# A product-key expert mixer: from gathered expert rows for all tokens to dense passes for three token tiles and gathered rows for two

## The chip, the cores and the metric

The kernel runs on one core of one Trainium2 chip. The metric is the device time of one execution in microseconds (us). Engines: PE (matrix multiply), DVE (VectorE), ACT (ScalarE), POOL (GpSimd), SP (issues DMAs).

## The reference, cut to what matters

The program is one step of a two-layer backbone over 640 tokens (128 context tokens, 512 latent tokens) of width 1024, all in float32. Each layer ends with an expert mixer over 16384 experts, each of which is one row of a table `u` and one row of a table `v`:

```
def peer(h, w_q, subkeys, u_tab, v_tab):
    q = (ht @ w_q).reshape(T, PEER_HEADS, 2, PEER_HALF)
    s = jnp.einsum('thpd,hpnd->thpn', q, subkeys)
    s1, i1 = lax.top_k(s[:, :, 0], PEER_TOPK)
    s2, i2 = lax.top_k(s[:, :, 1], PEER_TOPK)
    ...
    sc, pos = lax.top_k(cand, PEER_TOPK)
    eidx = jnp.take_along_axis(cidx, pos, axis=-1)
    gate = jax.nn.softmax(sc, axis=-1)
    def expert_block(args):
        xi, ei, gi = args
        a = jax.nn.gelu(jnp.einsum('td,tkd->tk', xi, u_tab[ei]), approximate=False)
        return jnp.einsum('tk,tkd->td', gi * a, v_tab[ei])
```

There are 8 heads, 128 keys per half (so expert = 128 i + j), and 16 experts per head: 128 picks per token, and 128 tokens per tile, 5 tiles. A row of either table is 4 KB, a whole table of one layer is 64 MiB (67.1 MB). The result is scaled by the layer's gate vector and added to the residual stream x.

## The kernel before, in words

The program is a row of stages (`build`), each closed by a barrier of all engines. In each layer the last two are `modulate` (normalises x into `h`, and PE turns `h` into `hT`) and `peer`. Everything outside `peer` is the same in both kernels but for one line of `modulate`.

`peer` of before works in 40 units, one for each tile and head. For one unit DVE chooses 16 experts per token: `select_subkeys` takes the best 16 of 128 scores for each half with `best16` (L1351 to L1355: MAX8, FIND_INDEX8, MATCH_REPLACE8, MAX8, FIND_INDEX8), and `select_experts` the best 16 of the 256 sums and their indices (L1363 to L1379). POOL then gathers rows (`gathers`, L1190 for u, L1194 for v): one indirect DMA fetches one row of 4 KB for each of the 128 tokens, 0.5 MB, into one of 8 slots for u and 8 for v. DVE multiplies each u row with the token's `h` and sums (`meet`, L1390), ACT applies the gelu, and DVE the gate (L1400). ACT makes a diagonal matrix of the 128 weights of each pick (L1240), and PE multiplies it with the gathered v rows and accumulates 16 picks in PSUM (`products`, L1303). DVE adds the sum to x (`add_y`, L1411 and L1414). The units are pipelined: the scores and the choice of unit n+1 lie in unit n. Most units are in hardware loops (`every`), in which each semaphore value is held in a register (`hold`).

Queries come first: PE turns the keys (L1330), and makes the queries of the context tile for all heads (L1338, weights loaded on SP in rows of 2 KB), and later the other 4 tiles' queries chunk by chunk between the products (L1313, weights `w_later` loaded on SP in rows of 512 bytes).

In all, each layer issues 640 gathers of u and 640 of v on POOL.

## Time and profile before

| | |
|---|---|
| median of 3 runs | 5233.46 us (5231.72 to 5237.55) |
| span of the profiled execution | 5232.4 us |
| its own time beside its span | shown nowhere but by the median: 1.1 us more |
| instructions | 51066 |
| busy PE, DVE, ACT, POOL | 3918.3, 3046.2, 1093.8, 3138.9 us |
| bytes read from HBM, written | 1476.98 MB, 3.48 MB |
| of these by POOL's gathers | 1342.42 MB, 2560 DMAs |

The trace is of one profiled execution. Busy time is the time in which an engine executes; a DMA's issue on POOL is counted as busy there. "PEclk" is the clock that PE was granted, 1.0 for 2.4 GHz and 0.5 for 1.2 GHz. "DMA share" is the mean busy share of the core's 16 DMA engines. "Releaser" is what ended an idle stretch of an engine; "issue" means that the profile shows nothing that it waited for.

### The profile page before, as it was taken

The numbers are of one execution on the slowest core, as the hardware profiler recorded it, in microseconds if no ns is written. First come the engines' busy times: TensorE is split into PE (matmuls) and PEld (weight loads), VectorE is DVE, ScalarE is ACT, GpSimd is POOL, SyncE is SP. The second block draws the span as 40 slices with busy tenths as digits, with TensorE's granted clock in tenths as the row PEclk, the third lists the DMA queues.
The fourth block names the chain that finished last, engine by engine and source line by source line (L and its number), as shares of the span: only waits on it lengthen the run. The fifth ranks groups of instructions, "written<-read, shape, count | busy, mean of one in ns | idle before, by whom it ended". The sixth has DMA issues, their size and how long they took to land. (4 is left out here: it accounts for less than half of the span.)

```text
span 5232.4 us, 51066 instructions
## 1 busy us (share of the span) xinstructions
PE 3918.3 (75%) x11340; PEld 1901.7 (36%) x11340; DVE 3046.2 (58%) x6901; ACT 1093.8 (21%) x2566; POOL 3138.9 (60%) x2832
## 2 busy tenths in 40 slices
PE   8986787787787666676678898877787666766675
PEld 3544754333333222232233443533333223322232
DVE  2014744766666666666651552666666666667665
ACT  1002212212221222122211242222222221222222
POOL 0003603777777777777760331477777777777775
PEclk9998888898898888888888799888889888888888
DMA  4126017999999999999992401899999999999997
GB/s 159 58 64 175 4 36 267 387 364 361 362 362 359 354 356 358 359 357 353 356 346 77 121 1 32 315 381 365 363 363 354 359 358 364 356 353 359 357 359 302
DMA packets 525836, 1482.66 MB, mean 283 GB/s; under 512 B 52901, under 2 KB 162597, under 8 KB 525513
## 3 DMA queue, kind: packets, MB, share of 16 engines
q0 software_dynamic: 369216, 1342.42, 68.7%
q1 hardware_dynamic: 154352, 138.22, 8.2%
q8 instruction: 58, 0.95, 0.1%
q14 instruction: 130, 1.06, 0.1%
q10 hardware_dynamic: 2080, 0.01, 0.0%
HBM read 1476.98 MB, written 3.48 MB: 283 GB/s over the span
## 5 line engine op out<-in xcount | busy, mean ns | idle before, releaser
L1303 PE MATMUL ps<-arena,mod_scale 128*128 128x512 f32 x5120 | 2472.0, 645 | 1030.4 <-ACT mod_scale L1240 1027.8
L1303 PEld LDWEIGHTS ps<-arena,mod_scale 128*128 128x128 f32 x5120 | 1051.5, 208 | 2414.9 <-issue 2324.7
L1190 POOL DMA_INDIRECT arena<-in_peer_u,small x1280 | 1381.3, 1079 | 726.3 <-issue 377.8
L1194 POOL DMA_INDIRECT arena<-in_peer_v,small x1280 | 1503.0, 1174 | 470.1 <-issue 317.8
L1390 DVE CUSTOM_DVE_ANT_0 arena<-arena 128x1024 f32<-128x1024 f32 x1280 | 1518.2, 1223 | 412.7 <-DMA arena<-in_peer_u,small 290.7
L1240 ACT ACTIVATE mod_scale<-ident,tail 128x128 f32<-128x128 f32 x1280 | 391.4, 388 | 82.3 <-DVE tail L1400 82.3
L1400 DVE TENSOR_TENSOR tail<-tail,small 128x8 f32<-128x8 f32 x160 | 27.0, 169 | 500.6 <-ACT tail L1236 499.9
L268 POOL TENSOR_TENSOR arena<-arena 2x512 f32<-2x512 f32 x12 | 15.5, 1294 | 464.4 <-ACT arena L260 464.4
L1236 ACT ACT_TABLE_LOAD x80 | 102.6, 1283 | 864.1 <-DVE tail L1390 863.9
L1228 ACT ACTIVATE arena<-ps 128x256 f32<-128x256 f32 x80 | 30.6, 382 | 1073.7 <-PE ps L1293 1073.7
L1313 PE MATMUL ps<-hT 128*128 128x512 f32 x512 | 231.6, 606 | 11.6 <-DMA hT<-in_peer_w_q 11.6
L1232 ACT ACT_TABLE_LOAD x80 | 102.6, 1283 | 560.3 <-DVE tail L1368 560.1
L527 PE MATMUL ps<-hT,arena 128*128 128x512 f32 x384 | 198.5, 599 | 2.1 <-PEq L70 2.1
L249 PE MATMUL ps<-hT,silu_c 128*2 128x128 f32 x1152 | 138.1, 280 | 43.9 <-DMA hT<-in_w_mod 43.0
L1785 POOL TENSOR_TENSOR arena<-arena,small 128x640 f32<-128x640 f32 (+3 forms) x80 | 76.2, 954 | 157.1 <-DVE small L1829 157.1
L1017 PE MATMUL ps<-arena,hT 128*128 128x512 f32 x320 | 141.8, 606 | 3.9 <-PEq L70 3.9
L1313 PEld LDWEIGHTS ps<-hT 128*128 128x128 f32 x512 | 97.1, 195 | 126.0 <-issue 110.8
L548 DVE COPY arena<-ps 128x640 f32<-128x640 f32 x12 | 9.9, 824 | 205.0 <-PE ps L528 205.0
L249 PEld LDWEIGHTS ps<-hT,silu_c 128*2 128x2 f32 x1152 | 95.8, 87 | 87.2 <-DMA hT<-in_w_mod 57.3
L1411 DVE TENSOR_TENSOR ps<-ps,mod_gate 128x1024 f32<-128x1024 f32 x80 | 98.5, 1231 | 41.8 <-PE ps L1303 32.7
L1351 DVE MAX8 small<-arena 128x8 f32<-128x128 f32 (+1 forms) x240 | 80.8, 337 | 65.3 <-ACT arena L1228 44.6
L1414 DVE TENSOR_TENSOR x<-x,ps 128x1024 f32 (+1 forms) x80 | 97.7, 1221 | 29.0 <-DVE ps L1411 28.6
(221 smaller groups left out, 3611.4 us busy)
## 6 DMA issues: line engine op xcount, KB each, us to landing
hT<-in_w_mod SPq DMA_DIRECT2D x144, 256.0 KB, 3.8
arena<-in_peer_u,small POOLq DMA_INDIRECT x1280, 6.3
arena<-in_peer_v,small POOLq DMA_INDIRECT x1280, 6.4
arena<-in_even_w_in SPq DMA_DIRECT2D x8, 2048.0 KB, 8.9
arena<-in_peer_w_q SPq DMA_DIRECT2D x8, 2048.0 KB, 11.6
hT<-in_peer_w_q SPq DMA_DIRECT2D x32, 512.0 KB, 15.0
arena<-in_w_mod SPq DMA_DIRECT2D x6, 2048.0 KB, 8.5
arena<-in_odd_w_in SPq DMA_DIRECT2D x3, 2048.0 KB, 14.1
```

The costliest lines, as they stand in the source:

```text
L249: mm = pe.matmul(self.m.ps[0:2, at % self.BANKS, c % 4 * P:(c % 4 + 1) * P], self.m.cT[:, k0 + k, :], self.ring[:, slot, k, :], start=(k0 ...
L527: pe.matmul(m.ps[:, b, :], lhsT, m.hT[:, k, 0:512], start=first, stop=end)
L1017: mm = pe.matmul(m.ps[:, i % 8, :], m.hT[:, k, t * P:(t + 1) * P], slots[n][:, k, :], start=(k == 0), stop=(k == KD - 1))
L1190: pool.indirect_dma_start(u_rows[:, j], None, u_table, at).then_inc(m.u_landed[j], 16)
L1194: pool.indirect_dma_start(v_rows[:, j], None, v_table, at).then_inc(m.v_landed[j], 16)
L1232: nc.scalar.activation(exps, sel, ACT.Exp, bias=neg_max, accum_out=exp_sum).then_inc(S.exp_ready, 1)
L1236: nc.scalar.activation(active[:, q], dots[:, q], ACT.Gelu).then_inc(S.gelu_ready, 1)
L1240: nc.scalar.activation(diag[:, q, j], m.ident[:], ACT.Copy, scale=weight[:, q, j:j + 1])\
L1303: mm = pe.matmul(y_banks[b][:, c], diag[:, q, j], v_rows[:, j, c * 512:(c + 1) * 512], start=(q == 0 and j == 0), stop=(q == 1 and j == HA ...
L1313: mm = pe.matmul(later_bank[i], w_later[:, k], m.hT[:, k, P:s.N], start=(k == 0), stop=(k == s.KD - 1))
L1390: dve.tensor_tensor_reduce(u_rows[:, j], u_rows[:, j], h_cur[:, b], 1.0, 0.0, ALU.mult, ALU.add, dots[:, q, j:j + 1]).then_inc(S.dotted, 1)
L1411: dve.tensor_tensor(share, share, mod, ALU.mult).then_inc(S.y_gated, 1)
```

## The change

`peer` is written anew. Tiles 0 and 1 (context and first latent tile) still go by gathered rows, 128 picks each, 256 picks per layer; tiles 2 to 4 (384 tokens) go dense over all 16384 experts, in 128 groups of 128 experts (group i holds experts 128 i + j). Both go on at once, interleaved in an order that is written out step by step (no loops are left, and all waits are on constants).

- **Prelude.** The queries of all five tiles are made 128 columns at a time by PE (`project`), followed by the scores (`score`) of all tiles; DVE chooses for tiles 0 and 1 (`choose`, `decode`). `decode` does for all 8 heads at once what was done per head.
- **First half, 128 steps in 4 stages of 32.** In step i SP loads 128 rows of u (4 DMAs of 32 partitions, rows of 1 KB), DVE transposes them in 32 x 32 blocks (`turn`), PE multiplies with `hT` of 384 tokens (`dots_of`), ACT applies the gelu and stores the 128 x 384 activations in DRAM (`act_rows`). In stages 0 to 2 DVE also makes one choice every 4 steps (tiles 2, 3, 4); at the start of stages 1 to 3 it decodes one tile; in stages 1 to 3 it makes, for 8 tokens at a time, one-hot matrices of i and j (`one_hot`, 128 x 1024 each, 48 groups), ACT multiplies one by the gate (`apply_gate`, 8 of 128 x 128), PE multiplies the two (`place_gates`), ACT copies the result out (`gates_out`), and stores it for two groups at a time, 1 MB, in DRAM (`gate_rows`).
- **Second half, 128 steps.** SP loads v (2 groups, 1 MB, rows of 4 KB), the activations (4 groups, rows of 1.5 KB) and the gates (8 groups, 1.6 MB, rows of 512 bytes); DVE multiplies activations by gates (`weigh`, 128 x 384), PE multiplies with v into 6 banks of PSUM (6 products of 128 x 512 a step).
- **Gathers beside both.** `pace` says how many picks are met by each step: 1.5 a step in stages 0 and 3, 0.25 in stages 1 and 2, 1.3 in the second half; the v rows follow 14 picks later. `meet` is as before. For tile 0 ACT scales each v row (`scale_row`) and POOL adds it; for tile 1 DVE does both in one (`add_row`). There are 8 slots for u and 4 for v. 512 gathers per layer.
- In `modulate` PE turns every eighth column of `h` instead of blocks of 128, and the query weights are loaded to match.

```diff
-                    mm = pe.transpose(m.ps[:, i % 8, j * P:(j + 1) * P], m.h[:, t, k * P:(k + 1) * P], m.ident[:])
+                    part = m.h[:, t, k * P:(k + 1) * P] if half == 0 else m.h[:, t, k::KD]
+                    mm = pe.transpose(m.ps[:, i % 8, j * P:(j + 1) * P], part, m.ident[:])
...
+LAG = 14
+def pace(i):
+    stage, r = divmod(i, STAGE)
+    if i < 0:
+        return 0
+    if stage == 0:
+        return max(0, 3 * (r - 1) // 2)
+    if stage in (1, 2):
+        return 45 + 8 * (stage - 1) + (r + 1) // 4
+    if stage == 3:
+        return 61 + 3 * (r + 1) // 2
+    return 109 + 13 * (i - STEPS + 1) // 10
...
+def rows_by(i):
+    return max(0, min(pace(i - 1) - LAG, P * GATHERED))
...
+            for k in range(PICKS + LAG):
+                if k + U_ROWS == P:
+                    pool.wait_ge(S.decoded, 2)
+                if k + U_ROWS < PICKS:
+                    pool.wait_ge(S.dotted, k + 1)
+                    u_gather(k + U_ROWS)
+                p = k - LAG
...
+                elif p < P:
+                    pool.wait_ge(S.scaled, p + 1)
+                    c(pool.tensor_tensor(y_sum[:, 0], y_sum[:, 0], v_rows[:, p % V_ROWS], ALU.add))
+                else:
+                    pool.wait_ge(S.dve_added, p - P + 1)
+                if p + V_ROWS < PICKS:
+                    v_gather(p + V_ROWS)
...
+                if n % 4 == 0:
...
+                    if g >= 2:
+                        sp.wait_ge(S.weighed, GBLOCK * (g - 1))
+                    sp.dma_start(g_in[:, g % 2].rearrange("p g i t -> p g (i t)"),
+                                 m.gate_rows[0:TG, :, g * GBLOCK:(g + 1) * GBLOCK, :].rearrange("g j i t -> j g (i t)"))\
+                        .then_inc(S.g_landed[g % 2], 16)
...
+                if n >= 2:
+                    sp.wait_ge(S.tile_done, VBLOCK * (n - 1))
+                sp.dma_start(v_in[:, n % 2], v_dense[n]).then_inc(S.v_landed[n % 2], 16)
...
+            for i in range(LAST):
+                if i + 2 < STEPS:
+                    turn(i + 2)
+                if i < STEPS:
+                    stage, r = divmod(i, STAGE)
+                    if stage >= 1 and r == 0:
+                        decode(GATHERED + stage - 1, best[0])
+                    for n in groups_at(i):
+                        one_hot(n)
+                    if head_at(i) is not None:
+                        t, h = head_at(i)
+                        choose(GATHERED + t, h, best[0])
+                if STEPS - 2 <= i < 2 * STEPS - 2:
+                    weigh(i - STEPS + 2)
+                for half in halves_by(i - 2):
+                    weights(half)
+                for p in range(picks_by(i - 1), picks_by(i)):
+                    meet(p)
+                for p in range(max(P, rows_by(i - 1)), max(P, rows_by(i))):
+                    add_row(p)
```

Three places of the order. First POOL in `peer` of the first layer. `L1190` and `L1194` are the gathers of u and v rows of before (`L1160` is the loop over units, `L1041` its register arithmetic):

```order
L1190 DMA arena<-in_peer_u,small 128x1024 x8
L1194 DMA arena<-in_peer_v,small 128x1024 x8
L1160 UNCONDITIONAL_BRANCH
L1160 ISA
L1041 ISA
L1190 DMA arena<-in_peer_u,small 128x1024
L1041 REGISTER_ALU
```

After the change, from the first gather on (`L1262` gathers u, `L1266` gathers v, `L1289` adds a scaled v row of tile 0 to the sum):

```order
L1262 DMA arena<-in_peer_u,small 128x1024 x8
L1266 DMA arena<-in_peer_v,small 128x1024 x4
L1262 DMA arena<-in_peer_u,small 128x1024 x15
L1266 DMA arena<-in_peer_v,small 128x1024
L1262 DMA arena<-in_peer_u,small 128x1024
L1289 TENSOR_TENSOR mod_shift<-mod_shift,arena 128x1024
L1266 DMA arena<-in_peer_v,small 128x1024
```

Runs of eight gathers have become single ones, each behind its own wait, with an addition between them for all of tile 0; the register arithmetic is gone.

Second DVE in the second half, tile 0 (`L1607` is `weigh`, `L1580` is `meet` with its read of the sum, `L1587` the gate on eight dots):

```order
L1607 TENSOR_TENSOR arena<-arena 128x384
L1580 ISA arena,tail<-arena,h 128x1024
L1580 ISA tail 128x1
L1607 TENSOR_TENSOR arena<-arena 128x384
L1587 TENSOR_TENSOR tail<-tail,arena 128x8
L1580 ISA arena,tail<-arena,h 128x1024
L1580 ISA tail 128x1
```

The sixteen `meet` of a unit, which stood in two runs of eight, now stand one or two at a time between the steps of the dense pass.

Third SP at the turn from the first half to the second (`L1219` loads u, `L1239` gates, `L1249` activations, `L1254` v):

```order
L1219 DMA arena<-in_peer_u 32x4x256 x500
L1239 DMA arena<-gate_rows 128x24x128
L1249 DMA arena<-act_rows 128x4x384
L1254 DMA arena<-in_peer_v 128x2x1024 x2
L1249 DMA mod_scale<-act_rows 128x4x384
L1254 DMA arena<-in_peer_v 128x2x1024 x2
L1239 DMA arena<-gate_rows 128x24x128
```

SP had 18 loads in `peer` of a layer; it now has 512 for u and, in the second half, 112, in this pattern.

## Rows read from the trace of the kernel before

**Rows 1.** The page: busy times of the engines; GB/s in 40 slices.
```profile
PE 3918.3 (75%) x11340; PEld 1901.7 (36%) x11340; DVE 3046.2 (58%) x6901; ACT 1093.8 (21%) x2566; POOL 3138.9 (60%) x2832
GB/s 159 58 64 175 4 36 267 387 364 361 362 362 359 354 356 358 359 357 353 356 346 77 121 1 32 315 381 365 363 363 354 359 358 364 356 353 359 357 359 302
```
**Rows 2.** Timeline, PE and DVE: first and last instruction of both peer stages (start us, us).
```profile
824.18 3.65 PE L1330 MATMUL ps<-ident,arena 128*128 128x128 f32 x16 [1.89 <-PEq L70]
2749.34 1.22 DVE L1414 TENSOR_TENSOR x<-x,ps 128x1024 f32<-128x1024 f32 x1
3289.54 3.33 PE L1330 MATMUL ps<-ident,arena 128*128 128x128 f32 x16 [1.94 <-PEq L70]
...
5210.01 1.22 DVE L1414 TENSOR_TENSOR x<-x,ps 128x1024 f32<-128x1024 f32 x1
```
**Rows 3.** Busy by stretch: length, engines, PEclk, DMA share, GB/s.
```profile
890.00:930.00 40.00, 33.34 (x74) 14.59 (x73) 28.43 (x67) 9.04 (x25) 30.55 (x32) 0.87 1.03 408
815.00:2755.00 1940.00, 1403.95 (x3272) 633.59 (x3272) 1274.08 (x3005) 412.00 (x1034) 1451.18 (x1280) 0.86 0.95 355
```
**Rows 4.** Groups of instructions, 3700 to 5000 us: busy us, mean ns, idle before.
```profile
L1390 DVE CUSTOM_DVE_ANT_0 arena<-arena 128x1024 f32<-128x1024 f32 x440 | 522.9, 1225 | 105.6 <-DMA arena<-in_peer_u,small 77.7 <-DVE small L1379 12.3 <-ACT arena L1222 9.2
L1194 POOL DMA_INDIRECT arena<-in_peer_v,small x441 | 508.1, 1152 | 168.6 <-issue 106.7 <-PE ps L1303 60.1 <-DVEq L1380 1.8
L1190 POOL DMA_INDIRECT arena<-in_peer_u,small x442 | 489.3, 1107 | 134.8 <-issue 130.8 <-PE ps L1303 4.0
```
**Rows 5.** Timeline, POOL: gathers on both sides of the start of a run of eight meets.
```profile
4301.64 0.95 POOL L1194 DMA_INDIRECT arena<-in_peer_v,small  x1 [0.30 <-PE ps L1303]
...
4305.18 1.99 POOL L1194 DMA_INDIRECT arena<-in_peer_v,small  x1 [0.30 <-issue]
```
**Rows 6.** Timeline, DVE, the same time: second and last of that run of meets.
```profile
4302.83 1.22 DVE L1390 CUSTOM_DVE_ANT_0 arena<-arena 128x1024 f32<-128x1024 f32 x1
...
4309.71 1.22 DVE L1390 CUSTOM_DVE_ANT_0 arena<-arena 128x1024 f32<-128x1024 f32 x1
```
**Rows 7.** Busy by stretch of 2 us, during and just after that run.
```profile
4304.00:4306.00 2.00, 0.00 (x0) 0.00 (x0) 2.00 (x5) 0.00 (x0) 1.70 (x2) 1.00 1.03 410
...
4310.00:4312.00 2.00, 0.00 (x0) 0.00 (x0) 0.93 (x2) 0.96 (x1) 1.75 (x1) 0.50 0.84 236
```
**Rows 8.** DMA issues: KB each, us to landing.
```profile
hT<-in_w_mod SPq DMA_DIRECT2D x144, 256.0 KB, 3.8
arena<-in_peer_u,small POOLq DMA_INDIRECT x1280, 6.3
...
hT<-in_peer_w_q SPq DMA_DIRECT2D x32, 512.0 KB, 15.0
```
**Rows 9.** Timeline, DVE: a choice outside the loops, its first instruction and the one behind it.
```profile
3308.11 0.30 DVE L1351 MAX8 small<-arena 128x8 f32<-128x128 f32 x1 [21.65 <-ACT arena L1228]
...
3314.98 0.15 DVE L1368 TENSOR_SCALAR tail<-small 128x1 f32<-128x1 f32 x1
```
**Rows 10.** Groups, 0 to 900 us, PE: products of 512 and of 128 columns.
```profile
L527 PE MATMUL ps<-hT,arena 128*128 128x512 f32 x384 | 198.5, 599 | 2.1 <-PEq L70 2.1
...
L528 PE MATMUL ps<-hT,arena 128*128 128x128 f32 x384 | 74.1, 275 | 0.0
```
**Rows 11.** Groups by shape, whole span: POOL and DVE, 640 or 1024 elements.
```profile
L1785 POOL TENSOR_TENSOR arena<-arena,small 128x640 f32<-128x640 f32 x32 | 40.1, 1252 | 55.5 <-DVE small L1829 55.5
...
L1414 DVE TENSOR_TENSOR x<-x,ps 128x1024 f32 x68 | 83.0, 1221 | 28.6 <-DVE ps L1411 28.6
...
L548 DVE COPY arena<-ps 128x640 f32<-128x640 f32 x12 | 9.9, 824 | 205.0 <-PE ps L528 205.0
...
L675 DVE TENSOR_SCALAR arena<-arena,small 128x640 f32<-128x640 f32 x8 | 4.4, 553 | 0.4
```
**Rows 12.** Groups by shape, 3700 to 5000 us, ACT.
```profile
L1240 ACT ACTIVATE mod_scale<-ident,tail 128x128 f32<-128x128 f32 x440 | 134.5, 388 | 29.2 <-DVE tail L1400 29.2
...
L1222 ACT ACTIVATE arena<-h 128x1024 f32 x25 | 26.0, 1042 | 0.0
```

More of the change, by code:

```diff
@@ L34, in __call__ @@
         self.n += 1
-        hold(self.engine, self.sem, self.offset + self.n, self.step)
+        self.engine.wait_ge(self.sem, self.n)
 class Shapes:
@@ new lines, with groups_at, head_at @@
+STAGE = 32
+STEPS = 4 * STAGE
+def groups_at(i):
+    stage, r = divmod(i, STAGE)
+    if not 1 <= stage <= 3 or not 2 <= r < 28:
+        return range(0)
+    first = 16 * (stage - 1)
+    return range(first + 16 * (r - 2) // 26, first + 16 * (r - 1) // 26)
+def head_at(i):
+    stage, r = divmod(i, STAGE)
+    return (stage, r // 4) if stage < 3 and r % 4 == 1 else None
+LAG = 14
+def pace(i):
+    stage, r = divmod(i, STAGE)
+    if i < 0:
[7 more added lines that the diff above has]
+    return 109 + 13 * (i - STEPS + 1) // 10
@@ L1196, in _ @@
[L1196 to L1210 removed]
+            c = Chain(pool, S.chain_p)
```

739 lines of the change are left out of this document (436 added, 303 removed).

## The prediction

> **What bounds the kernel now.** I read the page first, then stretches, then groups of instructions. The slices show two plateaus at about 360 GB/s with everything else between them [rows 1]. The timeline puts them in the two `peer` stages: 824.2 to 2750.6 us and 3289.5 to 5211.2 us [rows 2]. That is 1926 + 1922 us; outside them lie 5232.4 - 3848 = 1384 us, which the change does not touch. Inside, PE is busy 72% of the time, DVE 66%, POOL 75%, the DMA engines 95%, at 355 GB/s [rows 3]. So a layer costs what 1280 gathers of 0.524 MB (671 MB) cost. Two things set their rate, close together. The DMA engines can do 408 GB/s [rows 3]. POOL needs 0.95 us and 0.30 us before each one, 420 GB/s, but while DVE runs its meets back to back (one each 1.15 us [rows 6]) a gather takes POOL 1.99 us [rows 5]; the transfers go on from what is queued at 410 GB/s, and just after the run the rate is 236 with the DMA engines at 0.84 [rows 7]. Over 1300 us the mean is 1.13 us and 0.30 us, 1.43 us a gather [rows 4], 367 GB/s. POOL hardly waits for slots: 60 + 4 us for PE in that stretch [rows 4]. The bound is thus bytes, at a rate that POOL trims from 408 to 355.
>
> **What the change does to the bytes.** Per layer: 512 gathers, 268 MB; u and v dense, 67 MB each; activations written and read, 2 x 25 MB; gate table written and read, 2 x 25 MB. In all 503 MB behind the query weights, against 671. Engines get new work in exchange, so I cost each stretch by the longest of DMA, POOL and DVE.
>
> Prices. Gather on POOL 1.43 us [rows 4]. POOL's addition of 128 x 1024: 1252 ns for 640 elements scales to 2.0 us [rows 11]. Meet 1.15 us [rows 6]; other DVE passes with two inputs over 1024 elements 1.22 us [rows 11]. A choice: the one outside the loops takes 6.87 us to the instruction behind it, of which 0.2 us is a cast that moves into `decode`: 6.7 us [rows 9]. `decode`: 12 passes of 1024 elements at 1.26 us with their gaps and a dozen short ones, 18 us. One group of one-hots: 2 x 1.22 us and a gap, 2.5 us. PE: 512 columns 0.52 us, 128 columns 0.19 us (busy time by count [rows 10]), so 384 columns 0.39 us.
>
> The transposition of 128 x 1024 on DVE is in no row. Nearest from below is a one-input pass of 640 elements at 553 ns (0.9 us for 1024), at a rate of one element per cycle 824 ns (1.3 us) [rows 11]; from above two passes, 2.44 us. I take 1.22 us, as any full pass. The Trainium skill ("Vector Engine (DVE) Microarchitecture Reference", The reshape front-end and per-opcode configuration) says that a transposition sustains one element per cycle per lane, which would be my value; no row here shows it.
>
> **The sum, per layer.**
> - Prelude. PE: 16 chunks of 8 x (0.52 + 0.19) us and 1 us of scores, 107 us. Two choices come with each two chunks (13.4 us both on DVE and PE), so DVE ends 13 us later; then two turns and two decodes (39 us). 160 us in which only 12 MB move. Before, the first gathers ran 35 us after the start; this is the main new loss.
> - Stage 0 (32 steps): 45 picks met, 86 gathers, 68 MB with u and stores: at 370 GB/s 184 us. POOL 86 x 1.43 + 29 x 2.0 = 181. DVE 32 x 1.22 + 8 x 6.7 + 45 x 1.15 = 145. I take 185.
> - Stages 1 and 2: DVE 39 + 54 + 18 + 16 x 2.5 + 9 = 160 each, 165 with waits; DMA 40 MB, 109 us. PE, 256 x 0.39 + 128 x 0.19 = 124 us, hides.
> - Stage 3: 94 gathers, 81 MB: 218 us. POOL 94 x 1.43 + 47 x 2.0 = 228. DVE 152. ACT, 128 x 0.39 us for gates [rows 12], 47 rows at 1.04 us [rows 12] and copies, about 140. 230 us.
> - Second half: 298 gathers (156 MB), v 67, activations 25, gates 25: 274 MB. PE 768 x 0.52 = 400 us, DVE about 430, POOL 298 x 1.43 + 68 = 494: all hidden under DMA. Between 671 us (408 GB/s) and 780 (350) or more. I take 350: 782 us. The nearest row for mixed traffic is 355 [rows 3], and the rows of 512 bytes speak for the lower end (below).
> - The turn between the halves (gates must be stored, then 1.6 MB of them loaded before the first `weigh`) and the end, with the last 12 additions: 25 us.
> 160 + 185 + 330 + 230 + 782 + 25 = 1712 us, against 1924. The strided transposes of `modulate`, the unrolled code, and the 128 small stores on ACT I cost at nothing: ACT has some 90 us of room in stage 3 and more elsewhere, and without it a stage would grow by their issue. Total 1384 + 2 x 1712 = 4808 us on the span; the median before is 1 us above its span: **4810 us**.
>
> **The rivals.**
> 1. *The mixed queues do better than POOL's alone.* Half the bytes no longer need POOL's issue, so its 1.99 us behind DVE [rows 5] starves nothing, and DMA stays at 408 GB/s [rows 3]. Then stages 0 and 3 are POOL's (181, 228), 1 and 2 take 160 each, the second half 671, the ends 160 + 20: 1580 a layer, 4545 us. Against it: rows of 0.5 to 1.5 KB.
> 2. *DVE and POOL cost more.* If a turn takes 2.44 us, stages 1 and 2 grow by 39 us each. If each of POOL's additions waits out one two-input pass of DVE (1.22 us), as gathers visibly do [rows 5], stage 3 grows by 57 us and stage 0 by 35, since POOL sets them. Together 170 a layer: 5150 us. In what the trace shows, gathers lose 1.04 us to a busy DVE; the Trainium skill ("SBUF — State Buffer", SBUF: two separate sides) states such an exclusive lock between a DVE operation with two SBUF inputs and a GpSimd operation that reads SBUF. By that rule, which speaks against the additions placed on POOL, the sum would be 1804 a layer instead of 1712, by the price without a wait.
> 3. *Slower than before: SP's short rows starve beside the gathers.* The 256 KB loads of `w_mod`, alone, land in 3.8 us; the 512 KB loads with the same rows of 512 bytes beside gathers take 15.0 us [rows 8], 35 GB/s. The gate table is read in such rows, 1.6 MB each 8 steps, on the queue that v stands behind. If all of it goes at 35 GB/s it takes 720 us, and the other 92 MB of SP's at 290 another 318: 1038 instead of 782, 5320 us in all. It decides the sign once SP's 117 MB run below 118 GB/s on average (782 + 212 = 994 us). Against it: the gathers are paced by DVE, which waits when the gates are late; then at most 12 gathers (6.3 MB, 15 us) are left ahead, and SP has the engines alone. The Trainium skill ("DMA: Bandwidth & Descriptors", Queues, rings and completion order) says that a DMA engine takes turns between rings packet by packet; the 35 GB/s agree if a packet of the load is one short row.
> 4. *Not both at once.* Each waits on the other through DVE's fixed order, and the gathers add their 745 us (at 360) to dense passes without them: 160 + 146 + 165 + 165 + 155 + 336 + 745 + 25 = 1897, 5180 us. Against it: 8 slots are 5 steps of lead.
>
> **How the numbers follow.** Forecast 0.53, rival 1 0.22, rival 2 0.15, rival 3 0.06, rival 4 0.04. Runs of this kernel differ by 0.1%, so 0.2% (10 us) is about what can be told from no change. All cases but rival 3 are faster, though 2 and 4 come near: faster 0.92, same 0.02, slower 0.06. The range reaches from a little under rival 1 to rival 2: 4500 to 5160 us; it leaves out 3, 4 and the far tails.
>
> **What would show each step.** In the profile after: first gather about 140 us after the start of `peer`; stages 0 to 3 near 185, 165, 165, 230 us by the waits for stored gates; DVE over 90% busy in stages 1 and 2 with DMA share under 0.7; DMA share above 0.95 at 350 to 370 GB/s in the second half; a transposition of about 1.2 us; POOL's additions at 2.0 us. Wrong would be: a second half above 900 us with DVE or PE waiting for gates or v (rival 3), a turn of 2 us or more (rival 2), or a DMA share below 0.85 in stage 3 or the second half with no engine full, which would mean latency between engines, priced nowhere above.

## The result and the profile after

| | before | after |
|---|---|---|
| median of 4 runs | 5235.51 us (5231.72 to 5242.11) | 5448.35 us (5443.81 to 5449.32) |
| span of the profiled execution | 5232.4 us | 5447.3 us |
| HBM read, written | 1476.98 MB, 3.48 MB | 1024.00 MB, 104.14 MB |

The changed kernel is **slower**: ratio 1.0407, 95% interval 1.0392 to 1.0422. The forecast was 4810 us, in the range of 4500 to 5160 us. A quarter of the bytes (read and written) are gone and the time is 4% longer.

The page of the changed kernel, the lines that answer to [rows 1]:

```profile
PE 4484.1 (82%) x14942; PEld 2481.8 (46%) x14942; DVE 3209.8 (59%) x5185; ACT 1190.8 (22%) x2158; POOL 2080.0 (38%) x1558
GB/s 162 61 79 136 4 81 64 130 287 206 168 138 168 258 318 331 369 366 362 359 240 72 106 1 93 39 151 291 189 170 138 162 275 329 329 358 371 360 356 227
```

One plateau of about 360 GB/s per layer is left, the second half of the steps. Before it lie slices at 64 to 290 GB/s. Busy time by stretch for the first layer, cut where the stages begin (columns as in [rows 3]: PE, PEld, DVE, ACT, POOL, then PEclk, DMA share, GB/s). The rows are prelude, stages 0 to 3, second half:

```profile
828.00:1037.00 209.00, 166.83 (x704) 100.91 (x702) 136.30 (x446) 27.13 (x39) 11.44 (x12) 0.91 0.19 58
1037.00:1239.00 202.00, 172.73 (x500) 99.18 (x501) 187.31 (x327) 43.57 (x60) 130.38 (x85) 0.94 0.97 270
1239.00:1505.00 266.00, 210.88 (x768) 135.19 (x767) 186.65 (x303) 101.67 (x210) 66.94 (x44) 0.91 0.57 179
1505.00:1768.00 263.00, 214.00 (x773) 137.51 (x772) 181.48 (x301) 97.07 (x205) 37.36 (x24) 0.91 0.48 152
1768.00:2043.00 275.00, 208.66 (x756) 133.65 (x754) 215.41 (x178) 141.00 (x250) 223.20 (x137) 0.90 0.93 288
2043.00:2817.00 774.00, 670.86 (x1483) 292.31 (x1484) 432.37 (x575) 42.68 (x53) 439.72 (x340) 0.92 0.98 353
```

To be seen here: in stages 1 and 2 **nothing is full**. PE is busy 80% of them, DVE 70%, the DMA engines half. The second half is as forecast, at 0.98 and 353 GB/s. Stage 0 is full on two sides, DVE at 93% and DMA at 0.97, but this 0.97 moves only 270 GB/s.

Who waits for whom in stages 1 and 2 (waits, 1239 to 1768 us; us in total, times, longest):

```profile
DVE arena L1571 <- PE ps L1333: 147.0, 34, 9.3
ACT arena L1410 <- PE ps L1333: 137.2, 37, 7.3
...
PE ps L1350 <- ACT arena L1429: 64.4, 24, 3.9
...
PE ps L1340 <- DVEq L1552: 38.8, 2, 22.5
```

DVE waits 147 us with its next transposition (L1571) for PE's dots (L1333). PE waits 103 us for what starts on DVE: 64 us for one-hots that ACT scales (L1429), 39 us for the two decodes. Each waits for the other. The groups of stage 1 (1239 to 1505 us) give the prices:

```profile
L1333 PE MATMUL ps<-hT,arena 128*128 128x384 f32 x509 | 174.4, 502 | 0.5 <-DVE arena L1571 0.5
...
L1571 DVE STREAM_TRANSPOSE arena<-arena 128x1024 f32<-128x1024 f32 x32 | 64.9, 2032 | 71.7 <-PE ps L1333 71.4 <-DVE h L1545 0.2
L1350 PE MATMUL ps<-arena,mod_scale 128*128 128x128 f32 x256 | 39.7, 320 | 32.2 <-ACT arena L1429 32.2
```

The program issues 8 products of 384 columns a step, 256 in a stage, and the trace holds 509 of 512 records: **a float32 product is two matmul records**. (The matmuls' mean of 502 ns overlaps; 174.4 us of busy time over 256 products is 0.68 us for each.) The same holds in [rows 10]: 24 chunks of 8 products are written and x384 stands.

The prelude's chunks show the same without any wait (timeline, PE: products of 512 and 128 columns, one chunk's scores, and the next chunk's):

```profile
951.23 0.38 PE L1312 MATMUL ps<-hT,arena 128*128 128x128 f32 x2
951.45 1.02 PE L1311 MATMUL ps<-hT,arena 128*128 128x512 f32 x2
952.31 0.38 PE L1312 MATMUL ps<-hT,arena 128*128 128x128 f32 x2
952.53 1.28 PE L1324 MATMUL ps<-mod_shift,arena 128*128 128x128 f32 x10
...
962.30 1.28 PE L1324 MATMUL ps<-mod_shift,arena 128*128 128x128 f32 x10
```

A pair of products begins every 1.08 us (951.23 and 952.31) and a chunk takes 9.77 us, where the forecast had 6.7. The Trainium skill ("FP8 and Floating Point Precision", TensorE Precision Notes) says that true float32 goes through the PE array in 4 passes. The trace agrees: from the start of a product of 512 columns to that of the next behind it are 0.86 us (951.45 to 952.31), and 4 x 512 columns at the 2.4 GHz of a granted clock of 1.0 make 0.85 by this estimate.

### The profile page after: what moved, and what is told of

The parts are those of the page before. It is cut to its first block and busy times, and to the rows that moved or that the text cites. A ratio compares the mean times of both kernels' runs of the same rounds, so it can differ in the third digit from the quotient of the medians.

```text
span 5447.3 us, 44192 instructions
## 1 busy us (share of the span) xinstructions
PE 4484.1 (82%) x14942; PEld 2481.8 (46%) x14942; DVE 3209.8 (59%) x5185; ACT 1190.8 (22%) x2158; POOL 2080.0 (38%) x1558
## 3 DMA queue, kind: packets, MB, share of 16 engines
q8 instruction: 120, 1.97, 0.2%
HBM read 1024.00 MB, written 104.14 MB: 207 GB/s over the span
## 5 line engine op out<-in xcount | busy, mean ns | idle before, releaser
L1333 PE MATMUL ps<-hT,arena 128*128 128x384 f32 x4096 | 1410.1, 505 | 142.3 <-DVE arena L1571 140.7
L1333 PEld LDWEIGHTS ps<-hT,arena 128*128 128x128 f32 x4096 | 806.0, 200 | 698.3 <-DVE arena L1571 154.3
L1262 POOL DMA_INDIRECT arena<-in_peer_u,small x512 | 559.8, 1093 | 1285.9 <-DVE tail L1580 762.9
L1381 PE MATMUL ps<-arena 128*128 128x512 f32 x1536 | 727.7, 637 | 229.3 <-DMA arena<-in_peer_v 227.6
L1266 POOL DMA_INDIRECT arena<-in_peer_v,small x512 | 634.5, 1239 | 608.6 <-DVE mod_shift L1600 480.1
L1571 DVE STREAM_TRANSPOSE arena<-arena 128x1024 f32<-128x1024 f32 x256 | 520.7, 2036 | 404.9 <-PE ps L1333 402.7
L1580 DVE CUSTOM_DVE_ANT_0 arena<-arena,h 128x1024 f32<-128x1024 f32 x512 | 756.7, 1496 | 0.7 <-DVE h L1545 0.4
L1289 POOL TENSOR_TENSOR mod_shift<-mod_shift,arena 128x1024 f32<-128x1024 f32 x254 | 618.7, 2436 | 248.9 <-ACT arena L1457 244.5
L1381 PE MATMUL ps<-arena,mod_scale 128*128 128x512 f32 x1536 | 666.5, 593 | 2.6 <-DVE mod_scale L1607 2.4
L1381 PEld LDWEIGHTS ps<-arena,mod_scale 128*128 128x128 f32 x1536 | 292.1, 190 | 371.9 <-issue 367.2
L1607 DVE TENSOR_TENSOR arena<-arena 128x384 f32<-128x384 f32 x128 | 84.7, 662 | 598.0 <-DMA arena<-act_rows 598.0
L1350 PEld LDWEIGHTS ps<-arena,mod_scale 128*128 128x128 f32 x1536 | 231.7, 237 | 251.6 <-ACT arena L1429 246.6
L1429 ACT ACTIVATE arena<-arena,h 128x128 f32<-128x128 f32 x768 | 234.4, 388 | 284.9 <-DVE arena L1564 281.3
## 6 DMA issues: line engine op xcount, KB each, us to landing
arena<-gate_rows SPq DMA_DIRECT2D x32, 1536.0 KB, 21.2
```

The source lines that it names most:

```text
L1262: pool.indirect_dma_start(u_rows[:, p % U_ROWS], None, u_table, at).then_inc(m.u_landed[p % U_ROWS], 16)
L1266: pool.indirect_dma_start(v_rows[:, p % V_ROWS], None, v_table, at).then_inc(m.v_landed[p % V_ROWS], 16)
L1289: c(pool.tensor_tensor(y_sum[:, 0], y_sum[:, 0], v_rows[:, p % V_ROWS], ALU.add))
L1333: mm = pe.matmul(m.ps[:, i % 4, 0:ND], u_turned[:, i % 2, k], m.hT[:, k, N0:N], start=(k == 0), stop=(k == KD - 1))
L1350: mm = pe.matmul(m.ps[:, 6 + half, c * P:(c + 1) * P], hot_j[:, n % 2, tok], hot_i[:, n % 2, tok], start=True, stop=True)
L1381: mm = pe.matmul(m.ps[:, o, :], w_in[k // ABLOCK % 2][:, k % ABLOCK, t * P:(t + 1) * P], v_in[:, k // VBLOCK % 2, k % VBLOCK, half * 512:( ...
```

## The experiments

The first theories: **A**, PE's price per product was halved in the forecast, and the first half runs at PE's pace; **B**, DVE's dear transposition (2.04 us instead of 1.22) sets it; **C**, POOL's additions and DVE's passes block each other (rival 2). **D** was formed after the first four runs: with two buffers for the transposed u, each step costs the longer of DVE's and PE's work in it.

All stage times below are means of the two layers in us, from the timeline: the prelude begins with the first product of the queries (3.4 us after the start of `peer`), a stage with DVE's transposition in its first step, the second half with the first `weigh`. "Total" is the measured time of one execution, beside which the kernel before took 5234 to 5245 us; for the changed kernel and the last two rows it is the median of four. Executions of one of these kernels lay up to 32 us apart, so a smaller difference of two totals says little by itself; the stage times of the two layers lie within 10 us of each other in each execution, but for one place that is named at the end.

| kernel | prelude | 0 | 1 | 2 | 3 | second half | end | total |
|---|---|---|---|---|---|---|---|---|
| forecast | 160 | 185 | 165 | 165 | 230 | 782 | 25 | 4810 |
| changed kernel | 210 | 203 | 267 | 262 | 275 | 775 | 32 | 5448 |
| half of the dots | 210 | 196 | 242 | 236 | 268 | 775 | 30 | 5310 |
| no gates made | 210 | 202 | 194 | 189 | 249 | 795 | 29 | 5135 |
| short transposition | 210 | 191 | 228 | 221 | 266 | 778 | 30 | 5250 |
| four buffers | 210 | 196 | 208 | 202 | 273 | 774 | 31 | 5184 |
| four buffers, half dots | 209 | 197 | 191 | 185 | 268 | 775 | 31 | 5122 |
| no additions on POOL | 210 | 205 | 253 | 252 | 249 | 761 | 32 | 5334 |
| both of these: four, no additions | 209 | 194 | 200 | 200 | 242 | 762 | 30 | 5082 |
| half of the queries | 163 | 205 | 267 | 261 | 275 | 775 | 32 | 5358 |
| pace alone | 209 | 203 | 299 | 293 | 274 | 674 | 34 | 5373 |
| four buffers and pace | 210 | 196 | 228 | 221 | 270 | 674 | 33 | 5068 |
| + third choice early | 222 | 205 | 209 | 224 | 272 | 676 | 34 | 5090 |
| + 32, 24, 40 picks | 223 | 203 | 216 | 224 | 238 | 678 | 33 | 5029 |
| four buffers, 28, 28, 40 | 209 | 196 | 243 | 236 | 241 | 667 | 33 | 5055 |

### Half of the dots

```diff
-                for k in range(KD):
+                for k in range(KD // 2):
```

> Leaves out the second half of the sum in every dot of the dense first half: PE makes 4 instead of 8 products of 384 columns per step (5.33 us of PE per step becomes 2.67 us), nothing else changes. Theory A (the first half runs at PE's pace, since a float32 product is two matmuls, plus what PE waits for in its own order): stages 1 and 2 fall from 266 and 263 us to about 185 each, stage 0, where DVE is over 90% busy, stays near 200 us, stage 3 loses under 20 us; in all about -160 us per layer, near 5130 us. Theory B (the dear turn of 2.04 us and longer passes on DVE set the first half): stages 1 and 2 lose under 15 us each, above 5380 us. Theory C (POOL and DVE block each other): no change beyond 1%.

Stages 1 and 2 lost 26 us each, not 80, and the total came to 5310 us instead of 5130. Theory A in its plain form falls: PE's work in them shrank by 68 us and the time by 26. So does B, which had under 15. Busy time of stages 1 and 2:

```profile
1238.00:1479.00 241.00, 143.46 (x508) 98.51 (x509) 187.30 (x303) 100.42 (x209) 65.52 (x41) 0.77 0.64 192
1479.00:1714.00 235.00, 145.78 (x516) 98.03 (x515) 182.21 (x301) 96.92 (x205) 38.91 (x24) 0.80 0.57 170
```

Now PE is busy 60%, DVE 78%, and still DVE waits 93 us for PE's dots (27 times) and PE 125 us for the scaled one-hots (30 times). No engine's sum is the bound. Half of the products should have spared PE 87 us of stage 1's 174, and the edit spared PE 67 us in all: the mean granted clock fell from 0.91 to 0.77, as PE stood idle more often, and a product of 384 columns kept PE busy for 0.76 us instead of 0.68.

### No gates made

```diff
-                pe.wait_ge(S.gated, n + 1)
...
-                        mm = pe.matmul(m.ps[:, 6 + half, c * P:(c + 1) * P], hot_j[:, n % 2, tok], hot_i[:, n % 2, tok],
...
-                    e = nc.scalar.activation(one, one, ACT.Copy, scale=chosen[:, 2, at:at + 1])
...
-                c(dve.tensor_tensor(hot_j[:, n % 2], chosen[:, 1, toks].unsqueeze(2).to_broadcast(grid), axis,
```

> Leaves out the making of the gate table's content (48 groups per layer: two one-hots on DVE, 8 scalings on ACT, 8 products on PE, 2 copies on ACT); the stores and loads of the table remain, with whatever lies there, so the bytes are the same. Per group PE is spared 2.0 us and DVE 2.9 us, and with them the chain DVE, ACT, PE in which PE stands in its own order. Theory A with the chain as its second part: stages 1 and 2 fall from 266 and 263 us to about 180 (PE's 171 us of dots and the decode), stage 3 little. If only DVE's busy time counted, each stage would lose about 16 x 2.9 = 46 us: 220. If only PE's busy time counted, 16 x 2.0 = 32 us: 232. Total near 5110 us for the first, near 5270 us for the last two.

Stages 1 and 2 fell by 73 us each, to 194 and 189: more than DVE's 46 us or PE's 32 us of spared work alone, about as much as both together (78). That is what two engines that take turns would give. The edit also leaves out ACT's scaling between them, which this run can't tell apart. The second half took 20 us more, in its first 32 steps; that wasn't followed up.

### Short transposition

```diff
-                dve.transpose(u_turned[:, i % 2].rearrange("p c (m a) -> p m c a", m=4),
-                              u_raw[:, i % U_SLOTS].rearrange("p m (b c) -> p m c b", b=32)).then_inc(S.u_ready, 1)
+                part = 4 if i < 2 else 1
+                dve.transpose(u_turned[:, i % 2].rearrange("p c (m a) -> p m c a", m=4)[:, 0:part, 0:8 if i < 2 else 1],
+                              u_raw[:, i % U_SLOTS].rearrange("p m (b c) -> p m c b", b=32)[:, 0:part, 0:8 if i < 2 else 1]).then_inc(S.u_ready, 1)
```

> Leaves out nearly all of each transposition of u on DVE (from the third on, one block of 32 columns in place of 32 blocks; PE then multiplies old data): 2.04 us becomes about 0.1 us per step. Theory B (DVE's turn is the mis-sized term that made the kernel slower): stages 0, 1 and 2 lose about 60 us each, 200 to 140 and 265 to 205, total near 5080 us. Theory A: stage 0 stops at PE's 32 x 5.33 = 171 us (-30), stages 1 and 2 lose only what DVE adds to PE's waits, under 30 us each, total 5270 to 5380 us.

5250 us, just below A's range and far from B's: stage 0 lost 12 us only, stages 1 and 2 lost 39 and 41 of 60 us taken from DVE. DVE was left busy 127 us of stage 1's 229 and PE 197. So B isn't the bound, yet two thirds of each us taken from DVE count in stages 1 and 2, and 0.4 of each taken from PE (26 of 68, above).

### Four buffers for the transposed u

```diff
+    turned = [u_turned[:, 0], u_turned[:, 1], m.hT[:, :, 0:P], m.hT[:, :, P:2 * P]][:4]
...
-                    mm = pe.matmul(m.ps[:, i % 4, 0:ND], u_turned[:, i % 2, k], m.hT[:, k, N0:N], start=(k == 0),
+                    mm = pe.matmul(m.ps[:, i % 4, 0:ND], turned[i % 4][:, k], m.hT[:, k, N0:N], start=(k == 0),
...
-                if i >= 2:
-                    dve.wait_ge(S.dots_full, i - 1)
+                if i >= 4:
+                    dve.wait_ge(S.dots_full, i - 3)
```

The two new buffers are the columns of `hT` that belong to tiles 0 and 1, which nothing reads once the queries are made.

> Four buffers instead of two for the transposed u, so that DVE may run four steps ahead of PE's dots instead of two. Theory A in its strong form (PE is the bound and never short of work but for the gate chain): the waits move from DVE to PE, stages 1 and 2 fall towards PE's busy 211 us only if PE now finds its gates and turned rows ready, because DVE reaches the one-hots and the decode earlier: 225 to 240 us each, total 5300 to 5360 us. If instead the gate chain (one-hots, scaling, placing, in PE's own order) is a loop that the turn buffers have no part in: unchanged within 10 us per stage. Theory B: unchanged.

The same work, **265 us less** (5448 to 5184 us), and about 1% below the kernel before, whose executions lay between 5232 and 5248 us. Stages 1 and 2 at 208 and 202 us are lower than the strong form of A had them. The waits in them (1236 to 1645 us) and the stretches (stages 1, 2):

```profile
PE ps L1341 <- DVEq L1553: 26.4, 2, 21.6
DVE hT L1572 <- PE ps L1334: 21.1, 9, 3.1
...
DVE arena L1572 <- PE ps L1334: 8.2, 4, 3.3
```
```profile
1236.00:1444.00 208.00, 186.39 (x740) 121.36 (x740) 186.86 (x304) 101.25 (x209) 66.15 (x43) 0.94 0.78 227
1444.00:1645.00 201.00, 196.24 (x771) 127.22 (x770) 178.44 (x301) 96.80 (x206) 37.53 (x24) 0.98 0.67 199
```

DVE's waits for PE fell from 147 to 29 us, and PE's for the scaled one-hots from 64 us to none that is listed. PE is now busy 98% of stage 2, at a granted clock of 0.98. In stage 1 the trace lacks 28 of PE's 768 matmul records, so that its 186 us are some 7 us low; there PE (then 193 us) and DVE (187) are each busy 90 to 93% of 208 us, and PE still waits 26 us for the two decodes.

How two buffers made this can be read step by step in the changed kernel. PE and DVE, two timelines of stage 1, in the first of which PE waits for ACT's scaling and in the second DVE for PE:

```profile
1450.50 2.05 PE L1350 MATMUL ps<-arena,mod_scale 128*128 128x128 f32 x16 [1.89 <-ACT arena L1429]
1452.39 5.33 PE L1333 MATMUL ps<-hT,arena 128*128 128x384 f32 x16
1457.55 1.95 PE L1350 MATMUL ps<-arena,mod_scale 128*128 128x128 f32 x16
1459.33 10.49 PE L1333 MATMUL ps<-hT,arena 128*128 128x384 f32 x32
1473.35 1.86 PE L1350 MATMUL ps<-arena,mod_scale 128*128 128x128 f32 x7 [3.53 <-ACT arena L1429]
```
```profile
1452.18 1.23 DVE L1564 TENSOR_TENSOR arena<-h 128x1024 f32<-128x1024 f32 x1
1457.82 2.06 DVE L1571 STREAM_TRANSPOSE arena<-arena 128x1024 f32<-128x1024 f32 x1 [4.41 <-PE ps L1333]
1459.80 0.26 DVE L1498 MAX8 h<-arena 128x8 f32<-128x128 f32 x1
...
1466.42 2.03 DVE L1571 STREAM_TRANSPOSE arena<-arena 128x1024 f32<-128x1024 f32 x1
```

DVE may not transpose for step i+2 before the dots of step i are done. At 1453.4 us it stands 4.4 us for that. Then comes a choice of 6.6 us, in which PE uses up the two steps it has; and the one-hots of the next group, which lie behind the choice and the wait on DVE, are late for PE at 1469.8 us, by 3.5. The 4.4 us that DVE had stood could not be used to get ahead: the cheap steps on DVE (4.4 us with a group) can't pay for the dear ones (11 us with a choice) when the lead is a step. A step costs what the slower of the two needs in *that* step.

An estimate from the prices of the traces agrees in the main. Per step PE needs 5.33 us, with a group 2.0 more; DVE needs 2.04 us, with a group 2.5, a choice 6.6, a meet 1.3 and a decode 18 us more. The longer of the two, added up step by step, makes 246 us a stage; the longer of the two sums makes 203. Measured are 267 and 262 us with two buffers, and 208 and 202 with four. Some 20 us of the first pair are thus not this term; the additions on POOL (below) are worth 10 to 14 of them.

### Four buffers and half of the dots

Both edits above together.

> Four buffers, and half of the sum in each dot left out (4 of 8 products), which with two buffers took only 26 us off stages 1 and 2 where I had expected 80. New theory D: with two buffers DVE may only be one step ahead of PE, so each step costs the larger of the two engines' work in it (DVE: 2 to 13 us, PE: 5.3 to 7.4 us), and neither's sum is the bound; with four buffers the sums are. Then PE's sum, 188 and 205 us with all products, sets stages 1 and 2 now, and with half of them DVE's sum does: about 190 each, -15 us per stage and no more, since DVE's 187 us stand; total near 5120. If PE's sum were still not the bound: unchanged at 208 and 201.

As theory D had it, 5122 us and 191 and 185 us:

```profile
1233.00:1425.00 192.00, 127.14 (x506) 86.69 (x507) 184.96 (x302) 101.25 (x210) 62.96 (x42) 0.85 0.83 244
1425.00:1610.00 185.00, 132.56 (x514) 88.56 (x513) 179.20 (x300) 96.58 (x205) 34.64 (x24) 0.86 0.75 215
```

DVE, with the same 185 us of work that filled 78% of stage 1 with two buffers, now fills 96%. D stands: with two buffers the steps couple; with four the sums count, and PE's and DVE's lie close together (193 and 187 us of stage 1's 208, 196 and 178 of stage 2's 201), so that neither alone gives much more. Other ways to loosen the steps (more buffers for the one-hots, a choice cut into pieces) were not tried.

### No additions on POOL, with two and with four buffers

```diff
-                    c(pool.tensor_tensor(y_sum[:, 0], y_sum[:, 0], v_rows[:, p % V_ROWS], ALU.add))
+                    pass
```

> Leaves out POOL's 127 additions of tile 0's scaled v rows per layer (2.44 us each), nothing else of the changed kernel; tile 0's sum is wrong by that. Theory C (rival 2 of the prediction: POOL's additions and DVE's passes with two inputs shut each other out): the meets, 1.50 us in the mean in stages 1 to 3, come down to 1.2 us, the one-hots too, and stage 3, where POOL is busy 223 of 275 us, loses 30 us or more; total -70 us per layer or more, near 5300. Theory D: stages 0 to 2 wait for something else and lose under 10 us together; stage 3 loses only what DMA, busy 0.93 of it, leaves: under 15 us; total above 5400.

5334 us lies between what C had (near 5300) and what D had (above 5400), nearer to C: stages 1 to 3 lost 14, 10 and 26 us, the second half 14, stage 0 nothing. Theory C is right too, beside D. The meets between 1768 and 2040 us, in the changed kernel (its stage 3) and without the additions (the last 229 us of stage 3 and the first steps of the second half; in its stage 3 alone, 1748 to 1997 us, the mean is 1211 ns):

```profile
L1580 DVE CUSTOM_DVE_ANT_0 arena<-arena,h 128x1024 f32<-128x1024 f32 x45 | 84.6, 1902 | 0.2 <-DVE h L1545 0.2
```
```profile
L1580 DVE CUSTOM_DVE_ANT_0 arena<-arena,h 128x1024 f32<-128x1024 f32 x55 | 65.4, 1212 | 0.2 <-DVE h L1545 0.2
```

One of these meets in stage 3 of the changed kernel, on DVE and on POOL (timelines):

```profile
1873.40 1.22 DVE L1580 CUSTOM_DVE_ANT_0 arena<-arena,h 128x1024 f32<-128x1024 f32 x1
...
1874.55 3.37 DVE L1580 CUSTOM_DVE_ANT_0 arena<-arena,h 128x1024 f32<-128x1024 f32 x1
...
1877.85 2.06 DVE L1571 STREAM_TRANSPOSE arena<-arena 128x1024 f32<-128x1024 f32 x1
```
```profile
1874.32 2.51 POOL L1289 TENSOR_TENSOR mod_shift<-mod_shift,arena 128x1024 f32<-128x1024 f32 x1
1877.11 1.65 POOL L1266 DMA_INDIRECT arena<-in_peer_v,small  x1 [0.27 <-POOL mod_shift L1289]
```

The addition ends at 1876.83, the meet at 1877.92: by its length of 1.2 us it began about when POOL was done. So **DVE waits out POOL's addition**, more than POOL waits for DVE. Over the whole trace the 141 meets that overlap an addition take 2.24 us in the mean and up to 3.89, the other 371 take 1.21; the 142 additions that overlap a meet or a one-hot pass take 2.49 us, the others 2.36. The transposition, with one input, isn't held up: 2.05 us for the 65 that overlap an addition by more than 0.5 us, 2.03 for the others.

The same with four buffers:

> Four buffers, pace unchanged, and POOL's 127 additions of tile 0 per layer left out. With two buffers, leaving them out took 15, 11 and 26 us off stages 1, 2 and 3 (and 10 us off the second half). Theory D with C as a separate term: with four buffers stages 1 and 2 (208 and 201 us) go by PE's sum, 188 and 205 us, so shorter passes on DVE give under 6 us each there; stage 3 (272 us) still loses 20 to 28 us, by DMA's busy share of 0.95 no more than to about 245. Sum per layer -35 to -50 us, total 5085 to 5115. If the two are the same term (DVE's lateness), stage 3 loses under 10 us now and the total stays above 5150.

5082 us, 3 us below the range of the two-term theory; stages 1 and 2 lost 8 and 2 us. Stage 3 lost 31 us again, so this blocking is a term of its own: alone the two edits are worth 265 and 115 us, together 366. Stage 3 then is the DMA engines':

```profile
1630.00:1873.00 243.00, 210.32 (x788) 132.68 (x787) 165.87 (x177) 142.30 (x254) 101.16 (x91) 0.95 0.99 333
```

### Half of the queries

The same edit in `project` (4 of 8 pairs of products).

> Leaves out half of the sum in the queries of the changed kernel's prelude (4 of 8 pairs of products of 512 and 128 columns per chunk), nothing else; the experts chosen are others, the work as much. Theory A for the prelude (PE sets its pace, at 9.76 us per chunk because each float32 product is two matmuls; my prediction had 6.7 us): PE needs 5.3 us per chunk, then DVE's two choices for each two chunks, 13.2 us, are the longer: 8 x 13.2 = 106 us, and the prelude falls from 210 us to 155 to 165, the rest of the layer stays. Total near 5350 us. If the loads of the query weights or DVE set the prelude: no change, 5448.

163 us, total 5358. PE's scores now stand 5.44 us apart (900.46, 905.90, 911.34), and DVE is busy 136 of 163 us. So 47 of the prelude's 50 us over the forecast go with PE's price.

### Another pace

```diff
-        return 45 + 8 * (stage - 1) + (r + 1) // 4
+        return 45 + 24 * (stage - 1) + 3 * (r + 1) // 4
...
-        return 61 + 3 * (r + 1) // 2
-    return 109 + 13 * (i - STEPS + 1) // 10
+        return 93 + 3 * (r + 1) // 2
+    return 141 + (i - STEPS + 1)
```

> Only the pace of the gathered picks is changed: 24 picks each in stages 1 and 2 instead of 8, 48 in stage 3 as before, so that 37 picks (74 gathers, 39 MB) leave the second half. The DMA engines were busy 0.57 and 0.48 of stages 1 and 2 and 0.98 of the second half. Theory A: where the dense steps and the gathers each wait for what the other engine has just done, added meets and row additions (16 x 1.25 us of DVE in stage 1, 32 x 1.25 in stage 2 at most) lengthen stages 1 and 2 by 20 to 35 us each; the second half falls from 775 us by 39 MB at 353 GB/s = 110 us to 665. Net -40 to -70 us per layer: total 5310 to 5370 us. If the second half is bound by PE (671 us busy) rather than by DMA, it stops at about 700: total near 5400.

5373 us, 3 us above the expectation. The second half gave 101 us, as bytes at 353 GB/s have it; stages 1 and 2 took 63 of them, although DVE's busy time there rose by 41 us in each and both DVE (228 of 299 us) and DMA (0.72) had room. With the coupling a filler costs what it takes.

The same pace with four buffers:

> Four buffers for the transposed u together with the pace of 24 picks in stages 1 and 2. With four buffers alone these stages took 208 and 201 us with DMA at 0.79 and 0.67, PE at 188 and 205 us, DVE at about 187. Expected: DVE grows by 20 to 40 us per stage and becomes level with PE or passes it, DMA reaches 1.0: stages 1 and 2 at 225 to 235 us; second half 665 to 700 us. Net against four buffers alone -25 to -60 us per layer: total 5060 to 5130 us, against 5245 before the change. If stages 1 and 2 grow by as much as the second half gives (each near 255), nothing is won: 5180.

5068 us, at the lower end of the expectation: with four buffers the same picks cost 20 us a stage and give 100. The second half, 674 us, is now near PE's sum too:

```profile
1960.00:2620.00 660.00, 635.88 (x1451) 278.79 (x1452) 351.73 (x489) 4.28 (x16) 243.65 (x239) 0.98 0.98 352
```

### The third tile's choices in the prelude, and 32, 24, 40 picks

```diff
-    return (stage, r // 4) if stage < 3 and r % 4 == 1 else None
+    if i == 1:
+        return 0, 7
+    if stage == 0:
+        return (1, r // 4) if r % 4 == 3 else None
+    return (2, r // 4) if stage == 2 and r % 4 == 1 else None
...
-                for t in range(GATHERED):
+                for t in range(GATHERED + 1 if h < H - 1 else GATHERED):
```

> Four buffers and the pace of 24 picks, and in addition the third tile's choices are made in the prelude, where DVE is busy 138 of 210 us (one third choice per head, 6.6 us, fits PE's 19.5 us per head beside the two others, 13.2 us); the fourth tile's move to stage 0, and stage 1 has none. Expected: prelude + 0 to 5 us, stage 0 the same 196 us, stage 1 loses 53 us of DVE's 216 and is then bound by PE (188 us) and DMA (0.90 of 222 = 200 us): 200 to 208 us, the rest the same. Total 5068 - 2 x 18 = 5032 us (5020 to 5060). If stage 1 is held by PE's gate chain instead, unchanged.

A miss: 5090 us, 22 us above the kernel without it and 58 above the expected 5032. Stage 1 lost 19 us as expected, but the prelude took 12 us more instead of 5 at most, and stage 0 took 9 more. I take it that DVE's room there, which lies between PE's chunks, is filled by three choices (19.8 us per head against PE's 19.5) with nothing left for the two transpositions among them; this wasn't tested. At the start of stage 0 PE has waited 57 us for DVE where it waited 44.

Then the pace, on top of that:

```diff
-        return 45 + 24 * (stage - 1) + 3 * (r + 1) // 4
+        return 45 + (r + 1) if stage == 1 else 77 + 3 * (r + 1) // 4
-        return 93 + 3 * (r + 1) // 2
+        return 101 + 5 * (r + 1) // 4
```

> As the kernel with the third choice in the prelude, with 32 picks in stage 1, 24 in stage 2 and 40 in stage 3 (8 picks, 8.4 MB, go from stage 3, where DMA is busy 0.96 at 298 GB/s, to stage 1). Expected: stage 3 loses 8.4 MB / 298 GB/s = 28 us (270 to about 243), stage 1 gains at most that, since it had DMA to spare: 215 to 225 us. Total 10 to 30 us below the kernel before it: 5010 to 5030 us. If stage 1 is DMA-bound already, the two cancel.

Stage 3 lost 36 us instead of 28, stage 1 gained 5 (209 to 214): 5018 us, inside the expectation and 72 us below the kernel that it is built on, since stage 1 had room for the picks and stage 3 none. The same kernel again, in four executions:

> The fastest kernel so far once more (four buffers, third choice in the prelude, picks 32, 24, 40 in stages 1 to 3), timed against the kernel before the change: 5018 us in one execution. Expected 5010 to 5030 us, ratio 0.958 with an interval of under 0.003; against the kernel without the third choice level within 20 us, since the prelude's 13 us and stage 0's 8 us stand against 20 us in stage 1.

**5029 us** (5027.38 to 5040.14), ratio to the kernel before **0.9607, 95% interval 0.9589 to 0.9625**. The first execution of 5018 us was a low one: with it, those of this kernel spread by 0.4%. Its stages 0 to 3 and second half, layer 0:

```profile
1048.00:1252.00 204.00, 179.65 (x512) 102.70 (x512) 196.61 (x354) 44.74 (x61) 135.52 (x89) 0.92 0.98 275
1252.00:1467.00 215.00, 183.26 (x724) 118.02 (x725) 202.98 (x152) 122.25 (x232) 173.18 (x104) 0.93 1.01 310
1467.00:1692.00 225.00, 203.10 (x780) 130.55 (x779) 219.08 (x334) 114.66 (x225) 119.01 (x75) 0.95 0.86 259
1692.00:1931.00 239.00, 206.30 (x781) 131.55 (x779) 197.62 (x163) 134.38 (x245) 197.58 (x119) 0.94 0.99 312
1931.00:2620.00 689.00, 653.05 (x1480) 286.62 (x1481) 360.21 (x501) 4.28 (x16) 250.11 (x242) 0.97 0.96 344
```

In every one of them an engine or the DMA engines are at 95% or more. What is left idle is the prelude (DMA 0.19 in the changed kernel).

And without the third choice in the prelude:

```diff
-        return 45 + 24 * (stage - 1) + 3 * (r + 1) // 4
+        return 45 + 28 * (stage - 1) + 7 * (r + 1) // 8
-        return 93 + 3 * (r + 1) // 2
+        return 101 + 5 * (r + 1) // 4
```

> Four buffers, no third choice in the prelude, and the pace 28 picks in stages 1 and 2, 40 in stage 3 (24, 24 and 48 took 228, 221 and 271 us). Stage 3 near 237 us as in the kernel with the third choice and that pace (-34); stages 1 and 2, where DVE is busy 216 and 217 us, gain 4 meets and up to 4 row additions each, 5 to 10 us of DVE: 235 and 230. Net -18 us per layer: 5030 us (5015 to 5050), ratio to before 0.961.

5055 us (5042.64 to 5074.51), ratio 0.9657, 95% interval 0.9626 to 0.9688: faster than before, but 25 us above my 5030. Stage 3 came as expected; stages 1 and 2 took 243 and 236 us, 15 us each for 4 picks, with DVE at 98%. By the rows it is C again: the meets of stages 1 and 2 took 1555 ns in the mean with 24 picks and 1836 ns with 28, the first of the two one-hot passes 1545 and 1796 ns, as more of POOL's additions fell beside them. The estimate had counted a meet as 1.2 us and forgot that a pick also brings an addition that DVE waits for.

## Why the prediction was wrong

The forecast missed by 638 us: 312 a layer, and some 14 outside the terms of the sum (the turning of the keys ahead of the first query, 3.4 us a layer, and 7 us between the layers). Two steps failed: PE's work was priced at half, and each stretch was costed by its longest engine although two of them move in step. By its own terms:

- **Prices, PE.** "512 columns 0.52 us, 128 columns 0.19 us (busy time by count)": this is the step that failed first, in the order of the sum. The count in [rows 10] is of records, two to a product, so every product on PE was priced at half. A step's dots cost 5.33 us, not 3.1; a chunk 9.77 us, not 6.7; a second-half step 5.2 us, not 3.1. The code would have told: it writes 192 products on each of the lines of [rows 10], half of what x384 says.
- **Prelude, 160 us.** Measured 210; 47 of the 50 us go with that price (halved products: 163). The part on DVE was right.
- **Stages 1 and 2, "165 with waits".** Measured 267 and 262, two thirds of the whole miss. "PE, 256 x 0.39 + 128 x 0.19 = 124 us, hides" is 203 us at the measured prices (32 x 5.33 + 16 x 2.0) and did not hide: some 38 us a stage. The larger part, 60 us a stage, is a term the sum did not have at all: "I cost each stretch by the longest of DMA, POOL and DVE", though `turn` waits for the dots of two steps before, so that no engine can carry work over from a dear step to a cheap one. Rival 4 named "each waits on the other", for gathers against dense steps; the place was the two buffers between DVE and PE. The text also said what would show it, "a DMA share below 0.85 in stage 3 or the second half with no engine full"; it didn't occur there, but in stages 1 and 2.
- **Transposition, 1.22 us.** Measured 2.04 us, between the taken value and the upper bound of 2.44; 26 us more of DVE a stage. In the changed kernel the whole transposition costs 40 us a stage in stages 1 and 2 and 12 in stage 0. The Trainium skill ("Vector Engine (DVE) Microarchitecture Reference", The reshape front-end and per-opcode configuration) gives one element per cycle per lane. The trace doesn't agree for this transposition of float32: at the rate that the forecast took for one element per cycle (640 elements in 824 ns, [rows 11]) 1024 would take 1.3 us.
- **Stage 0, 185 us.** Measured 203 (196 with four buffers), and near only by luck, since two errors stand against each other. It was costed at 370 GB/s, where its mix of gathers and u rows of 1 KB fills the DMA engines at 270 to 278; and it counted 86 gathers and 68 MB, where the trace has 62 gathers and 54 MB between 1041 and 1239 us. DVE was at 187 us, not 145.
- **Stage 3, 230 us.** Measured 275. Rival 2 had one mechanism of it and gave it 0.15: the additions and DVE's two-input passes shut each other out. The runs without additions give 26 to 31 us in stage 3 and nothing in stage 0 (205 us against 203, 194 against 196), where rival 2 had 57 and 35; stages 1 and 2, where it had none, give 10 to 14 us with two buffers and 2 to 8 with four. And it's mostly DVE that waits, so the meets show it (1.90 us) and the additions (2.44 us) only little. Without the additions stage 3 still takes 242 to 249 us: with the DMA engines at 0.99 it moves 333 GB/s, not the 370 of the sum.
- **Second half, 782 us.** Measured 775 at 353 GB/s: right, and for the reason given. PE is much nearer than thought (671 of 774 us busy instead of 400): its 768 products at 0.86 us make 660 us, under which fewer bytes give nothing. Rival 3, which held the whole chance of "slower", did not occur: the gate loads took 21.2 us to land for 1.5 MB, 74 GB/s, and DVE waited 302 us for the activations behind them, but the DMA engines were at 0.98 meanwhile.
- **The strided transposes of `modulate` and the small stores at nothing:** right as far as the traces show: a group of 8 transposes takes up to 1.97 us in both kernels, and between the layers the changed kernel takes only 7 us more.

So the sign was wrong though the bytes were right: bytes fell as said, and in the prelude and stages 1 and 2, 740 us of each layer, they are not the bound. It is the coupling that turned the sign: with four buffers and every other price as it is, the kernel takes 5184 us, 1% below before (one execution), while with half of the dots and two buffers it stays above, at 5310. The forecast's chance of 0.06 for slower rested on one mechanism in the second half, and none of the rivals questioned the price of PE, since the sum showed it hidden by a factor of 1.3 or more in every stage behind the prelude.

What stays open: why the kernel without gates takes 20 us more in the second half, and why the kernel with the third choice and 32, 24, 40 picks took 690 us for the second half of one layer and 668 for the other. Other places for tile 0's additions (DVE alone, or PE) were not tried.

## What to carry to other kernels

A new interleaving of two engines must be costed step by step against the depth of the buffers between them: sum the longer of both per step if the lead is one step, and only with a lead that spans the dearest step take the longer of the sums. Before moving work to an engine, check its price per *written* instruction (records in the trace over instructions in the code), and before filling idle DMA time with more work, find out whether the engines that handle it are coupled: the same 32 picks cost 63 us with two buffers and 39 with four, and the same program went from 4% slower to 3.4% faster than before by two spare buffers and another spread of the gathers.
